# Five input blocks of the second half moved from tile 0's dots into its sums, gate sums and shares set among the dots, and a denser attention with two wide evictions

## The reference

```python
q = (hf @ w_query).reshape(M, H, 2, PEER_DQ // 2)          # M = 512 rows, H = 8 heads
s = einsum('mhpc,hpnc->mhpn', q, sub_keys)                 # 2 x 128 scores a head
top_s, top_i = top_k(s, 16)
best_s, best_c = top_k((sums of all pairs), 16)            # 16 experts a head, 128 a row
g = softmax(best_s)
for each block of 128 rows:                                # blocks ("tiles")
    u = u_tab[ids]; v = v_tab[ids]                         # 128 x 128 rows of 1024
    act = gelu(einsum('nkd,nd->nk', u, x)) * g
    out = einsum('nk,nkd->nd', act, v)
```

## Time and profile before

| | us |
|---|---|
| median of three runs | 3093.45 (3090.16 to 3097.05) |
| the profiled execution's own time | 3091.62 |
| its span, first to last instruction | 3089.8 |
| busy PE, DVE, POOL, ACT | 1989.4, 1840.9, 1933.1, 279.4 |
| moved by the DMA engines | 1181.71 MB, 382 GB/s over the span |

### The profile page before, as it was taken

The page is one execution under the profiler, slowest core; times in us unless marked ns, Lnnn a source line. Parts: engine busy times, 40 slices in busy tenths (PEclk is TensorE's granted clock), DMA queues, the critical chain, the costliest instruction groups (busy, mean ns, idle before and its releaser), DMA issues.

```text
span 3089.8 us, 23884 instructions
## 1 busy us (share of the span) xinstructions
PE 1989.4 (64%) x7944; PEld 987.5 (32%) x7944; DVE 1840.9 (60%) x4796; ACT 279.4 (9%) x534; POOL 1933.1 (63%) x2053
## 2 busy tenths in 40 slices
PE   8899429977697409972299506993099205950299
PEld 6787302346341302442143301443043001210022
DVE  1249785298316899159715799338915799149700
ACT  3221000021000101200000100201000000000000
POOL 0014567666566677666666677666767777777675
PEclk9999759957899659996699757996599657985599
DMA  5248999999999999999999999999999999999998
GB/s 178 99 172 327 411 404 409 402 399 399 402 401 409 410 410 395 403 411 410 395 402 398 411 410 398 399 409 411 409 398 399 409 409 394 409 409 410 400 409 357
DMA packets 314043, 1181.71 MB, mean 382 GB/s; under 512 B 35760, under 2 KB 36288, under 8 KB 302400
## 3 DMA queue, kind: packets, MB, share of 16 engines
q0 software_dynamic: 294912, 1073.87, 87.7%
q1 hardware_dynamic: 19008, 106.31, 8.8%
HBM read 1177.95 MB, written 2.10 MB: 382 GB/s over the span
## 4 chain that ended last, share of the span: by engine, by line
PE 42%; DMA 34%; DVE 12%; POOL 7%; issue 4%; ACT 1%; SPq 0%; POOLq 0%; DVEq 0%; ACTq 0%
PE main_bank L362 31%; DMA main_ring<-in_u,main_idi 26%; DVE main_ring L328 9%; DMA main_ring<-in_v,main_id_by_slot 7%; PE main_bank L398 6%; POOL main_ring L293 6%; PE main_bank L396 2%; POOL main_ring L300 2%; PE main_bank L567 1%; PE main_bank L771 1%; PE main_bank L1174 0%; DVE main_resid L343 0%; DVE main_bank L320 0%; DVE main_att_s L958 0%; PE main_bank L755 0%
## 5 line engine op out<-in xcount | busy, mean ns | idle before, releaser
L293 POOL DMA_INDIRECT main_ring<-in_u,main_idi x1024 | 959.4, 937 | 689.4 <-DVE main_hid L328 332.2
L328 DVE CUSTOM_DVE_ANT_0 main_ring<-main_ring,main_bank 128x1024 f32<-128x1024 f32 x1024 | 1233.4, 1220 | 118.6 <-DMA main_ring<-in_u,main_idi 83.6
L300 POOL DMA_INDIRECT main_ring<-in_v,main_id_by_slot x1024 | 970.0, 947 | 449.1 <-PE main_bank L362 252.0
L362 PE MATMUL main_bank<-main_ring,main_lhs 128*32 128x512 f32 x4096 | 1145.8, 612 | 22.5 <-DMA main_ring<-in_v,main_id_by_slot 18.1
L352 PE MATMUL main_bank<-main_ident,main_act_out 128*128 128x128 f32 x8 | 3.8, 473 | 916.6 <-DVE main_act_out L338 916.6
L362 PEld LDWEIGHTS main_bank<-main_ring,main_lhs 128*32 128x32 f32 x4096 | 306.9, 110 | 789.8 <-issue 549.3
L398 PE MATMUL main_bank<-main_xT,main_w_block 128*128 128x256 f32 x1408 | 343.1, 397 | 15.7 <-ACT main_xT L434 9.8
L398 PEld LDWEIGHTS main_bank<-main_xT,main_w_block 128*128 128x128 f32 x1408 | 270.0, 197 | 111.8 <-issue 56.7
L352 PEld LDWEIGHTS main_bank<-main_ident,main_act_out 128*128 128x128 f32 x8 | 1.5, 182 | 918.7 <-DVE main_act_out L338 918.7
L343 DVE TENSOR_TENSOR main_resid<-main_bank,main_resid 128x1024 f32<-128x1024 f32 x8 | 9.8, 1225 | 392.9 <-PE main_bank L362 392.9
L153 DVE MAX8 main_top<-main_scores 128x8 f32<-128x128 f32 x128 | 28.3, 282 | 326.6 <-ACT main_scores L520 326.4
(11 more groups left out here) (203 smaller groups left out, 1267.6 us busy)
## 6 DMA issues: line engine op xcount, KB each, us to landing
main_w_block<-in_w_query SPq DMA_DIRECT2D x32, 1024.0 KB, 7.9
main_w_block<-in_w_ab SPq DMA_DIRECT2D x24, 1024.0 KB, 5.9
main_ring<-in_u,main_idi POOLq DMA_INDIRECT x1024
main_ring<-in_v,main_id_by_slot POOLq DMA_INDIRECT x1024
main_w_block<-in_w_c_in SPq DMA_DIRECT2D x16, 1024.0 KB, 8.4
main_w_block<-in_w_out SPq DMA_DIRECT2D x8, 1024.0 KB, 6.4
main_w_block<-in_w_c_out SPq DMA_DIRECT2D x8, 1024.0 KB, 7.9
main_att_bias<-in_att_bias SPq DMA_DIRECT2D x16, 256.0 KB, 5.2
```

The lines of the kernel that those rows point to most:

```text
L293: nc.gpsimd.indirect_dma_start(self.ring[n % self.bufs], None, self.u[p // NT], bass.IndirectOffsetOnAxis(self.choice.idi[:, p % 2, k:k + ...
L300: nc.gpsimd.indirect_dma_start(self.ring[n % self.bufs], None, self.v[p // NT], bass.IndirectOffsetOnAxis(self.idT[:, p % 2, t:t + 1], 0)) ...
L328: self.nc.vector.tensor_tensor_reduce(out=row, in0=row, in1=self.ps[:, 6:8], scale=1.0, scalar=0.0, op0=ALU.mult, op1=ALU.add, accum_out=s ...
L362: last = self.nc.tensor.matmul(self.ps[j * GROUP:(j + 1) * GROUP, 6 + a], self.lhs[:, t * GROUP:(t + 1) * GROUP], self.ring[n % self.bufs] ...
```

## The change

1. PE does blocks 0 to 6 of the second half (`LATE` = 7) and `z_pe` during tile 0's dots. The 80 pieces of blocks 7 to 11 go among tile 0's sums, five after every fourth row from row 8. ACT's evictions of these blocks go to the same place, after `put`. The gate's product gets bank 3 (`Z_BANK`), and the wait for all 12 evictions moves from it to the scores at row 80.
2. In every tile the sum of the exponentials goes after dot 114, the reciprocal after dot 117 and the product after dot 120.
3. In tile 1 a step of the attention follows every third dot instead of every fourth, and `OUT_AT` and the norm steps move forward.
4. `mix_turn_act` makes two evictions of 1024 columns instead of four of 512, in both halves.
5. In tiles 2 and 4 the last of the four evictions goes behind the Gelu, ahead of `put`.

```diff
+    def gate_sums(self, dve, p):
+        dve.wait_ge(self.exped, p + 1)
+        self.nc.vector.tensor_reduce(self.den[:], self.best[:], AX.X, ALU.add).then_inc(self.summed, 1)
+
+    def gate_shares(self, dve, p):
+        dve.wait_ge(self.summed, 2 * p + 1)
+        self.nc.vector.reciprocal(self.den[:], self.den[:]).then_inc(self.summed, 1)
+
     def gates(self, dve, p):
         nc = self.nc
-        dve.wait_ge(self.exped, p + 1)
-        nc.vector.tensor_reduce(self.den[:], self.best[:], AX.X, ALU.add).then_inc(self.summed, 1)
-        dve.wait_ge(self.summed, 2 * p + 1)
-        nc.vector.reciprocal(self.den[:], self.den[:]).then_inc(self.summed, 1)
         dve.wait_ge(self.summed, 2 * p + 2)
...
+    LATE = 7
...
+    Z_BANK, A_BANK, T_BANK, KV_BANK, O_BANK = (2, 3), ((2, 3), (0, 1)), (4, 2), ((5, 6), (3, 4)), ((4, 7), (2, 3))
...
+    def late_piece(self, pe, g, x):
+
+        self.in_piece(pe, g, self.LATE * self.w.PIECES + x)
...
     def z_pe(self, pe, g):
         pe.wait_ge(self.glr_there, g + 1)
-        if g:
-            pe.wait_ge(self.w.taken, self.FIRST[g] + self.IN)
...
     def gla_scores_pe(self, pe, g, t):
         if t == 0:
             pe.wait_ge(self.dec_there, g + 1)
+            if g:
+                pe.wait_ge(self.w.taken, self.FIRST[g] + self.IN)
...
     def mix_turn_act(self, act, g):
-        for k in range(4):
-            act.wait_ge(self.m_turned, 4 * g + k + 1)
-            self.nc.scalar.activation(self.mixT[g][:, 2 * k:2 * k + 2], self.ps[:, k].rearrange("p (a t) -> p a t", a=2),
+        for k in range(2):
+            act.wait_ge(self.m_turned, 4 * g + 2 * k + 2)
+            self.nc.scalar.activation(self.mixT[g][:, 4 * k:4 * k + 4], self.ps[:, 2 * k:2 * k + 2].rearrange("p b (a t) -> p (b a) t", a=2),
                                       ACT.Copy).then_inc(self.m_there, 1)
...
-OUT_AT = (85, 90, 96, 101)
+OUT_AT = (76, 82, 88, 94)
...
-                    for i in range(mix0.IN):
+                    for i in range(mix0.LATE):
                         mix0.in_act(act, 1, i)
...
                 experts.activate(act, p)
+                if p in (2, 4):
+                    mix1.act_x(act, hf, RT // 2 - 1)
                 experts.put(act, p)
                 if p == 0:
                     mix0.gla_logs_act(act, 1)
+                    mix0.in_act(act, 1, mix0.LATE)
                     mix0.gla_decays_act(act, 1)
+                    for i in range(mix0.LATE + 1, mix0.IN):
+                        mix0.in_act(act, 1, i)
...
-                        if k % 4 == 2 and k // 4 < 2 * AH + 3:
-                            mix0.att_dve(dve, 1, k // 4)
+                        if k % 3 == 2 and k // 3 < 2 * AH + 3:
+                            mix0.att_dve(dve, 1, k // 3)
...
-                        if k == 108:
+                        if k == 100:
                             norms.mean_dve(dve, 3)
-                        if k == 112:
+                        if k == 105:
                             norms.scale_dve(dve, 3)
...
-                choice.gates(dve, p)
+                    if k == 114:
+                        choice.gate_sums(dve, p)
+                    if k == 117:
+                        choice.gate_shares(dve, p)
+                    if k == 120:
+                        choice.gates(dve, p)
...
-                    for i in range(mix0.IN):
+                    for i in range(mix0.LATE):
                         mix0.in_pe(pe, 1, i)
...
+                    mix0.z_pe(pe, 1)
...
-                        if k == 4:
-                            mix0.z_pe(pe, 1)
+                        for x in share(k, 8, (mix0.IN - mix0.LATE) * weights.PIECES):
+                            mix0.late_piece(pe, 1, x)
```

More of the change, by code:

```diff
@@ L577 @@
     IN = 12
+    LATE = 7
     FIRST = (0, 24)
     BY_ROW = (2, 5, 8, 9, 10, 11)
-    A_BANK, T_BANK, KV_BANK, O_BANK = ((2, 3), (0, 1)), (4, 2), ((5, 6), (3, 4)), ((4, 7), (2, 3))
+    Z_BANK, A_BANK, T_BANK, KV_BANK, O_BANK = (2, 3), ((2, 3), (0, 1)), (4, 2), ((5, 6), (3, 4)), ((4, 7), (2, 3))
     BIASES = (0, 0, 0, 2, 3, 4, 6, 7, 8, 8, 8, 8)
@@ L674, in z_pe @@
         pe.wait_ge(self.glr_there, g + 1)
-        if g:
-            pe.wait_ge(self.w.taken, self.FIRST[g] + self.IN)
         for m in range(GPAIRS):
-            last = self.nc.tensor.matmul(self.ps[:, self.A_BANK[g][0], m * HALF:(m + 1) * HALF], self.w_alpha[:, m * P:(m + 1) * P],
+            last = self.nc.tensor.matmul(self.ps[:, self.Z_BANK[g], m * HALF:(m + 1) * HALF], self.w_alpha[:, m * P:(m + 1) * P],
                                          self.glr[0:GRANK], start=True, stop=True)
@@ L785, in out_wait_pe @@
     def out_wait_pe(self, pe, g):
-        pe.wait_ge(self.m_there, 4 * (g + 1))
+        pe.wait_ge(self.m_there, 2 * (g + 1))
     def in_act(self, act, g, i):
@@ L881, in gla_z_dve @@
         for m in range(GPAIRS):
-            last = nc.vector.tensor_scalar(self.zt[g][:, m], self.ps[:, self.A_BANK[g][0], m * HALF:(m + 1) * HALF], self.b_alpha[:, m:m + 1], None,
+            last = nc.vector.tensor_scalar(self.zt[g][:, m], self.ps[:, self.Z_BANK[g], m * HALF:(m + 1) * HALF], self.b_alpha[:, m:m + 1], None,
                                            ALU.add)
@@ L1031, in act_in, with act_x @@
         self.norms.gains_in(act, n, self.xT)
[L1032 to L1037, removed]
+        for i in range(RT // 2 - 1):
+            self.act_x(act, hf, i)
+    def act_x(self, act, hf, i):
+        b = self.FIRST[hf] + i
+        act.wait_ge(self.w.used, b + 1)
+        if i == 0 and hf:
+            act.wait_ge(self.carried, 2)
+        self.nc.scalar.activation(self.xb[:, 2 * i:2 * i + 2, CONV - 1:], self.w.result(b), ACT.Copy).then_inc(self.w.taken, 1)
     def act_gate_in(self, act, hf):
```

## The result

The changed kernel takes 3102.66 us, the median of 11 runs (3098.98 to 3106.11), beside 3091.58 us for the kernel before on the same chip (3087.12 to 3100.78). The ratio is 1.0032 with a 95% interval of 1.0022 to 1.0042: slower by 9.9 us, with 6.8 and 13.0 as the ends. (The medians themselves lie 11.1 us apart; this document reckons with the ratio.) The forecast was 6.1 us slower, 3099.5 us. The measured time lies in the range given, 3092.5 to 3104, but 0.9 us above the likeliest case's own upper end of 9.

A forecast was written before the change was run, and what follows sets the result against it. After the start the DMA engines were taken to set the time. Terms 0.8 - 3.0 + 8.1 + 0.4 = 6.3, less 0.2 for `z_pe`, gave +6.1 us on 3093.45: 3099.5 us, with an 8-in-10 range of 3092.5 to 3104.

The forecast's parts named there:

- likeliest case: Whole kernel: 6.1 us slower, with its own range of +3.5 to +9; chance 0.58.
- rival (b): Tile 0's sums: PE too late because of the five blocks, +8.4 us, or +10.7 with a second such loss; chance 0.12.
- The denser attention: Tile 1's dots: attention steps every third dot cost 8.1 us together, ends 2.6 and 10.
- room: Tile 1's dots: DVE's spare 0.14 us a dot, no longer found by the steps over 19 dots, 2.6 us lost.
- waits: Tile 1's attention: DVE waits 0.46 us for PE's scores at each of twelve steps, 5.5 us lost.
- The five blocks: Tile 0: five loads move from dots to sums; dots end 12.8 us earlier, sums 12.8 longer, net 0.
- the 0.8 taken for PE's pieces: Tile 0's sums: PE's work moved there loses 0.8 us, ends 0 and 3.1.
- The gates: Every tile's handoff from dots to sums: `weigh` starts 0.38 us earlier, 8 x 0.38 = 3.0 us gained, ends 0 and 3.0.
- Rival (c): Handoff returns more than given: 0.38 us earlier saves 1.9 us a tile, 15.2 in all, sum -6.1; chance 0.05.
- Rival (d): Handoff: gates within the dots gain nothing, as another wait on ACT or PE ends last; +9.1 us, chance 0.05.
- The wide evictions: At the start, the last eviction takes 1.03 us instead of 0.60: 0.43 us lost; nothing in tiles 1, 2 and 4.
- The clock (rival a): Tile 1's attention: PE's clock rises and the twelve DVE waits vanish, sum +0.6 us, 3094, not slower; chance 0.20.

The follow-up runs named there:

- two places: Changed kernel with attention output products alternating between two PSUM banks, steps still three dots apart: 3096.72 us, ratio 1.0007 to the kernel before.
- the longer handoff: Kernel before with four more reductions, read by nobody, ahead of the gates' sum in every tile's handoff: 3097.11 us, ratio 1.0009.
- two places in the kernel before: Kernel before with attention output products alternating between two PSUM banks, steps four dots apart as before: 3094.96 us, ratio 1.0002.

## Why the prediction was right, and the term that was off

The likeliest case had +3.5 to +9 us, and 9.9 came. That the time lies in the full range owes something to luck: its upper end was set by rival (b), which did not happen. On which side of 0.2% the result would fall was forecast at nearly even chances (0.48 the same, 0.46 slower); it is 0.32% slower.

**The denser attention: right in place, mechanism and size.** Worked out were 8.1 us, 2.6 of room and 5.5 of waits; the dots grew by 8.9, and the runs split them into 2.8 and 6.1. Alone it costs 7.4 us (5.0 to 10.2), and beside the other parts 9.9 - 1.2 = 8.7. The wait follows the dose: none at three dots with two places, 0.46 us at three with one, 1.60 at two. It was called 0.46 us for each of twelve steps, and that is what the trace has. The wait also stands in a PSUM bank and not in the clock or the loads, since a second bank alone removes it and changes nothing where there was no wait.

**The five blocks: right, net 0.** The dots end 13.7 us earlier, where 12.8 was worked out, the sums take 12.6 more, and alone the ratio is 1.0001. Tile 0's sums run at 406 GB/s, not under 404, so the 0.8 taken for PE's pieces doesn't show and neither does rival (b), a PE too late there. Its +8.4 to +10.7 is near what was measured, but its place is not: the loss is in tile 1's dots.

**The gates: the mis-sized term.** "Rows and POOL's next gather follow one for one, and DMA's idle time ends earlier by as much: 8 x 0.38 = 3.0 us gained." The first part holds nearly: in tile 0 the row comes 0.34 us earlier and POOL's next gather 0.33 (`weigh` follows the Gelu's end by 430.39 - 430.29 = 0.10 us instead of 0.07). POOL's pause is 0.25 us shorter there, and 0.33 with the gates alone. The step to DMA is the one that fails, in part. Gates alone gain 2.5 us with ends of 5.6 and -0.3, which doesn't contradict 3.0; but lengthening by twice as much costs 2.8 and not 6.1, tiles 6 and 7 give about half both ways, and beside the other parts no gain shows at all (+1.2 us without the attention, where -2.0 was forecast). At the value of the lengthening, 0.45 us for 1, the gates are worth 1.3 us instead of 3.0. Where the other half goes is not shown: tile 6's passage from sums to dots loses part of it, 403 instead of 409 GB/s, but the longer handoff gets nothing back there. Rival (c), five for one, is out: it had 15.2 us from the gates, their interval ends at 5.6, and 0.77 us more would have cost some 31. Rival (d), that nothing comes of it, stands at the edge of both intervals; its reason, another wait that ends last, is not there, since the row did come earlier.

**The wide evictions: right.** At the start 4.76 - 4.34 = 0.42 us, where 0.43 was worked out. It is passed on: from the first output product to tile 0's inputs are 36.33 us in eleven of the fourteen traces, the change without the denser attention among them. In the changed kernel's own trace they are 38.6, because the granted clock is 0.76 in the first 9.3 us of these products, where before had 1.00, and the first 64 matmuls take 16.31 us instead of 14.08; a trace with narrow evictions (two places in the kernel before, 38.5) has the same, with 0.77 and 16.19 us, so this is not the change's. In tiles 2 and 4 nothing shows on the first chips.

**The clock (rival a): fell.** It stayed at 0.50 in tile 1's attention from 650 to 690 us, with PE's pauses down from 1.40 to 0.73 us and PE busy 35.6 of 40 us, in matmuls of 64 rows or columns and transpositions; at two dots a step it was 0.50 as well. In tile 0's sums, with PE busy 177.35 of 180.81 us, it is 0.98. No trace of the first two chips shows more than 0.50 from 650 to 690 us, and none shows what would bring it there.

**The remaining 3.8 us** between 6.1 and 9.9: the change without the denser attention has 3.2 of them (+1.2 for -2.0), and the attention 0.6 (8.7 for 8.1). Of the 3.2 the gates' missing 1.7 is the largest piece that an experiment prices; the rest is within the interval of 3.1 to either side. The parts measured alone sum to -2.5 + 7.4 + 0.3 + 0.4 = 5.6 us, and the whole to 9.9; with about 3 us of uncertainty in each the two don't contradict each other, and whether the parts make each other worse stays open. What comes after tile 1 doesn't differ by more than single executions do.

## What to carry to other kernels

When helper work is packed closer within a stream that is near its limit, look at the round trip from one helper step to the next: where one buffer ties it to the other engine, the wait appears as soon as the spacing is shorter than this trip, here 5.07 us against 4.61 (at 5.75 there was no wait), and a second buffer takes it away again. A few tenths of a us won at a pause of the main stream can be worth less than their length, here about half, so price such a term by making the pause longer, which is easier to measure. And keep bursts whole where matmuls of different column quarters overlap, but no longer than the buffers cover: here pieces one at a time cost 11.9% and ten at a time 1.1%, against five.

## What the runs showed of the hardware

- One row's four matmuls of 128 x 32 weights take 1.90 us alone, and sixteen of four consecutive rows in the four column quarters 1.94 us, or 0.49 a row, both at a granted clock of 1.00. That is 3.9 times as fast when all four rows have landed, and one foreign matmul pair between the rows takes it all away: each row then takes 1.90 us, 2.46 us from one to the next.
- The kernel before ran 7% slower on another chip, and two kernels close to it show PE there issuing a matmul every 1.4 to 2.8 us in tile 0's dots and waiting for nothing in the profile. The sign of a change can turn there: the input products, which end 95 us before the dots do elsewhere, ended 33 us after them, and the change without its gates gained 32 us, where it costs about 10 elsewhere with them.
